# First attention in a two-block kernel: key/value groups side by side on half arrays, keys in two halves, values stationary

## What is computed

```python
def attend_blocks(q, k, v):            # q: (B, 512, 8, 64); k, v: (B, 768, 2, 64)
    ...
    scale = ATT_HEAD_DIM ** -0.5
    def one_block(qi):
        s = jnp.einsum("bqhgd,bkhd->bhgqk", qi, k, preferred_element_type=jnp.float32) * scale
        p = jax.nn.softmax(s, axis=-1)
        return jnp.einsum("bhgqk,bkhd->bqhgd", p.astype(v.dtype), v)
```

## Time and profile before

| | |
|---|---|
| median of 3 runs | 2099.91 us (2099.75 to 2102.64) |
| profiled execution | 2094.38 us, its span 2093.1 us |
| TensorE busy | 1808.2 us, 86% of the span |
| VectorE, ScalarE, GpSimd busy | 866.0, 547.3, 126.8 us |
| attention and scan stage | 155.8 to 539.9 us |
| mean granted TensorE clock | 0.958 of full speed |

### The profile page before, as it was taken

One profiled execution on the slowest core, in us unless ns is written; L12 is line 12 of the kernel. 1 busy time (PEld: TensorE's weight loads), 2 busy tenths in 40 slices (PEclk: granted clock), 3 DMA queues, 4 the chain that ended last, 5 costly groups with the idle time before them and its releaser, 6 DMA issues.

```text
span 2093.1 us, 21196 instructions
## 1 busy us (share of the span) xinstructions
PE 1808.2 (86%) x8537; PEld 1227.8 (59%) x8537; DVE 866.0 (41%) x1365; ACT 547.3 (26%) x908; POOL 126.8 (6%) x120
## 2 busy tenths in 40 slices
PE   4999889897899893888888888899788699999998
PEld 2657475766677771333232333488467678888876
DVE  4066372437733426011110111527567744444443
ACT  2134333334522313000000000232345533222221
POOL 0002120203000001000000000000000001000010
PEclk9999999998999996999999999999889899999999
DMA  9131202112104221999999999442300022232211
GB/s 348 55 109 41 82 20 101 41 72 90 41 1 167 104 98 52 384 421 421 421 422 422 421 420 420 150 156 85 121 1 1 1 81 81 82 120 81 81 41 41
DMA packets 92360, 329.44 MB, mean 157 GB/s; under 512 B 7348, under 2 KB 22632, under 8 KB 67688
## 3 DMA queue, kind: packets, MB, share of 16 engines
q1 hardware_dynamic: 84384, 312.59, 38.1%
q10 hardware_dynamic: 5928, 8.16, 1.2%
q0 software_dynamic: 1952, 7.34, 0.9%
HBM read 322.82 MB, written 4.19 MB: 156 GB/s over the span
## 4 chain that ended last, share of the span: by engine, by line
PE 66%; DMA 14%; DVE 12%; ACT 4%; issue 3%; ACTq 1%; POOL 1%; SPq 1%; DVEq 0%; POOLq 0%
PE PS L565 20%; PE PS L346 13%; PE PS L663 8%; PE PS L884 8%; DMA ring<-in_w_exp_down_dram 6%; DMA ring<-in_w_exp_gate_dram 5%; PE PS L342 3%; PE PS L534 3%; PE PS L674 2%; PE PS L729 2%; DVE wR L1415 1%; PE PS L772 1%; PE PS L426 1%; DMA ring<-in_w_mod_dram 1%; DVE mrow L1426 1%
## 5 line engine op out<-in xcount | busy, mean ns | idle before, releaser
L565 PE MATMUL PS<-hR,wR 128*128 128x512 f32 x1200 | 301.0, 410 | 30.9 <-DVE wR L1415 17.1
L565 PEld LDWEIGHTS PS<-hR,wR 128*128 128x128 f32 x1200 | 233.8, 197 | 95.6 <-issue 34.5
L663 PE MATMUL PS<-ring,xeT 128*64 128x512 f32 x1024 | 230.3, 600 | 40.3 <-DMA ring<-in_w_exp_gate_dram 38.0
L1415 DVE TENSOR_TENSOR wR<-ring,wR 128x1024 fp32r<-128x1024 f32 (+2 forms) x142 | 161.1, 1135 | 250.8 <-ACT wR L946 250.6
L946 ACT CAST wR<-ring 128x1024 fp32r<-128x1024 f32 (+2 forms) x142 | 138.3, 975 | 217.0 <-PE PS L884 126.5
L663 PEld LDWEIGHTS PS<-ring,xeT 128*64 128x64 f32 x1024 | 76.8, 138 | 192.5 <-issue 186.1
L884 PE MATMUL PS<-wR,hR 128*128 128x512 f32 x768 | 176.2, 390 | 8.9 <-DVE tmp L2097 6.9
L565 PE MATMUL PS<-xR,wR 128*128 128x512 f32 x768 | 175.3, 389 | 0.0
L884 PEld LDWEIGHTS PS<-wR,hR 128*128 128x128 f32 x768 | 143.6, 188 | 41.5 <-DVE tmp L2097 9.6
L565 PEld LDWEIGHTS PS<-xR,wR 128*128 128x128 f32 x768 | 144.1, 188 | 29.9
L663 PE MATMUL PS<-ring,hidT 128*64 128x512 f32 x512 | 115.2, 596 | 25.9 <-DMA ring<-in_w_exp_down_dram 20.0
(11 more groups left out here) (381 smaller groups left out, 2316.9 us busy)
## 6 DMA issues: line engine op xcount, KB each, us to landing
ring<-in_w_exp_gate_dram SPq DMA_DIRECT2D x64, 1024.0 KB, 13.9
ring<-in_w_exp_up_dram SPq DMA_DIRECT2D x64, 1024.0 KB, 13.7
ring<-in_w_exp_down_dram SPq DMA_DIRECT2D x64, 1024.0 KB, 11.9
ring<-in_w_mod_dram SPq DMA_DIRECT2D x12, 2048.0 KB, 8.6
ring<-in_w_in_dram SPq DMA_DIRECT2D x11, 2048.0 KB, 9.3
ring<-in_w_up_dram SPq DMA_DIRECT2D x8, 2048.0 KB, 8.3
ring<-in_w_down_dram SPq DMA_DIRECT2D x8, 2048.0 KB, 7.8
ring<-in_w_in_dram SPq DMA_DIRECT2D x9, 1024.0 KB, 5.5
```

The costliest lines, as they stand in the source:

```text
L565: mm = T.matmul(b, o[s][:, k, :], x[:, t, k, :], start=(k + j == 0), stop=(k == nk - 1 and j == 2))
L663: mm = T.matmul(b[es, ns], stat[:, 2 * kq + k, es], W.view(units[e2])[:, k, ns], start=(kq + k == 0), stop=(kq == 3 and k == 1))
L1415: V.tensor_tensor(lo, W.view(unit)[:, ks, cs], hi.bitcast(F32), ALU.subtract) \
```

## The change

Heads j of both groups now go side by side, 16 pairs instead of 32 heads. The keys lie in `kT`, both groups' channels one over the other, without zeros. Scores of a pair are two products with 64 partitions each, one on each half of the array's rows, for 384 of the keys; a second call does the other 384. VectorE takes the maxima of both heads in each half of the keys, and Exp uses the half's own maximum. `scale` then finds the smaller negative maximum, the Exp of each half's gap to it, the whole sum, its reciprocal, and scales P itself, in four pieces, before it is turned. Values are stationary (128 keys by 64 channels), turned P of two pairs moves (256 columns), one group on each half of the array's columns; the output comes with channels in partitions, so that it is copied to `oattT` at once and `ot` is gone. `oattT` has its channels in another order, and `head_cols` loads the rows of the second branch's matrix to suit, in two transfers. The attention has 66 turns again, in the order of `attention_order`.

```diff
...
@@ -104,7 +104,18 @@
 
 
 def cols(w, a, n):
-    return w[:, a:a + n].rearrange("(k p) n -> p k n", p=128), w.shape[0] // 128, n
+    k = w.shape[0] // 128
+    return [(slice(0, 128), slice(0, k), w[:, a:a + n].rearrange("(k p) n -> p k n", p=128))], k, n
+def head_cols(w, a, n):
+    parts = [(slice(64 * g, 64 * g + 64), slice(0, 4), w[256 * g:256 * g + 256, a:a + n].rearrange("(j p) n -> p j n", p=64))
+             for g in range(2)]
+    k = w.shape[0] // 128
+    if k > 4:
+        parts.append((slice(0, 128), slice(4, k), w[512:, a:a + n].rearrange("(k p) n -> p k n", p=128)))
+    return parts, k, n
 
 
 def weight_units(d):
...
@@ -119,8 +130,8 @@
                 u.append((("mod", 4 + 4 * hp + (0, 0, 0, 0, 0, 1, 2, 3)[n]),
                           *cols(d["w_mod"], 2048 + 512 * (4 * hp + what), 512)))
     u.append(("gate", *cols(d["w_in"], 2048, 512)))
-    for br, (a, wb) in enumerate(((3328, "w_branch_a"), (4352, "w_branch_b"))):
-        u += [(("wb", br), *cols(d[wb], 0, 1024)), (("mg", br, 0), *cols(d["w_in"], a, 512)),
+    for br, (a, wb, rows_of) in enumerate(((3328, "w_branch_a", cols), (4352, "w_branch_b", head_cols))):
+        u += [(("wb", br), *rows_of(d[wb], 0, 1024)), (("mg", br, 0), *cols(d["w_in"], a, 512)),
               (("mg", br, 1), *cols(d["w_in"], a + 512, 512))]
     u += [(("wo", s), *cols(d["w_out"], 512 * s, 512)) for s in range(2)]
     for p in range(8):
...
@@ -173,11 +184,10 @@
 
     m1 = Area(nc, KEEP, HT)
     oattT, oT = m1.take("oattT", [128, 4, 512]), m1.take("oT", [128, 4, 512])
-    qT, kz = m1.take("qT", [128, 4, 512]), m1.take("kz", [128, 2, 768])
-    pb = m1.take("pb", [128, 2, 768])
+    qT, kT = m1.take("qT", [128, 4, 512]), m1.take("kT", [128, 768])
+    pb, avs = m1.take("pb", [128, 2, 768]), m1.take("avs", [128, 6, 128])
     m2 = Area(nc, DYN, END)
-    avs, pT = m2.take("avs", [128, 6, 128]), m2.take("pT", [128, 2, 768])
-    ot, st = m2.take("ot", [128, 2, 512]), m2.take("st", [128, 4, 3])
+    pT, st = m2.take("pT", [128, 6, 2, 2, 128]), m2.take("st", [128, 2, 6, 2, 2])
     qh, vh = m2.take("qh", [128, 2, 512]), m2.take("vh", [128, 6, 256])
     KK, GG, LF = (m2.take(n, [128, 2, 768]) for n in ("KK", "GG", "LF"))
     lbt, reset = m2.take("lbt", [128, 6, 8]), m2.take("reset", [128, 768], U8)
...
@@ -406,7 +416,7 @@
         def turn_keys(pool):
             T.wait_ge(*dve_in["k"])
             for i in range(6):
-                b = pool.take(T, ("kT", i), act_in["kz", i])
+                b = pool.take(T, ("kT", i), act_in["kT", i])
                 turn(b[:, 0:128], akv[:, i, :]).then_inc(pe_in.sem, pe_in.up(("kT", i)))
 
         def turn_query(pool, i):
@@ -418,36 +428,34 @@
 
         def attention(pool):
             T.wait_ge(*act_in["qT", 3])
...
+            def scores(u):
+                n, kh = divmod(u, 2)
+                i, j = divmod(n, 4)
+                b = pool.take(T, ("s", u), act_att["e", u], 2)
+                for g in range(2):
+                    gs = slice(64 * g, 64 * g + 64)
+                    mm = T.matmul(b[:, 512 * g:512 * g + 384], qT[gs, j, 128 * i:128 * i + 128],
+                                  kT[gs, 384 * kh:384 * kh + 384], start=True, stop=True)
+                mm.then_inc(pe_att.sem, pe_att.up(("s", u)))
+            def turn_p(n, g):
+                b = pool.take(T, ("t", n, g), act_att["pT", n, g], 2)
+                T.wait_ge(*dve_att["sc", n])
+                for c in range(6):
+                    mm = turn(b[:, 128 * c:128 * c + 128], pb[:, g, 128 * c:128 * c + 128])
+                mm.then_inc(pe_att.sem, pe_att.up(("t", n, g)))
+            def values(n):
+                b = pool.take(T, ("v", n), act_att["o", n])
+                T.wait_ge(*act_att["pT", n, 1])
+                for c in range(6):
+                    for g in range(2):
+                        mm = T.matmul(b[64 * g:64 * g + 64, 0:256], avs[:, c, 64 * g:64 * g + 64],
+                                      pT[:, c, g].rearrange("p j q -> p (j q)"), start=(c == 0), stop=(c == 5))
+                mm.then_inc(pe_att.sem, pe_att.up(("v", n)))
+            yield from attention_order(scores, lambda n: None, turn_p, values)
 
         def scan(pool, level_pool):
             for q in range(4):
...
@@ -910,6 +918,25 @@
         select()
         ffn()
 
+    def attention_order(scores, scale, turn_p, values):
+        for n in range(17):
+            if n < 16:
+                scores(2 * n)
+            if n:
+                turn_p(n - 1, 1)
+            yield
+            if n < 16:
+                scores(2 * n + 1)
+                yield
+                scale(n)
+            if n and n % 2 == 0:
+                values(n - 1)
+            yield
+            if n < 16:
+                turn_p(n, 0)
+                yield
     def select_order(scores, compress2, compress3, mix_conv, turn_out, compressed, turn2, values2):
 
         steps = None
...
@@ -994,13 +1021,9 @@
                 A.activation(rr[:, 0:n], rr[:, 0:n], ACT.Sqrt).then_inc(s.sem, s.up(("rms", name)))
 
         def turn_keys():
-            A.wait_ge(*pool_in["kz"])
             for i in range(6):
                 A.wait_ge(*pe_in["kT", i])
-                for g in range(2):
-                    gs = slice(64 * g, 64 * g + 64)
-                    c = A.copy(kz[gs, g, 128 * i:128 * i + 128], bank(("kT", i))[gs, 0:128])
-                c.then_inc(act_in.sem, act_in.up(("kz", i)))
+                A.copy(kT[:, 128 * i:128 * i + 128], bank(("kT", i))[:, 0:128]).then_inc(act_in.sem, act_in.up(("kT", i)))
 
         def turn_query(i):
             A.wait_ge(*pe_in["qT", i])
...
@@ -1009,26 +1032,35 @@
 
         def attention():
             s = act_att
...
+            def scores(u):
+                n, kh = divmod(u, 2)
+                A.wait_ge(*dve_att["max", u])
+                if n:
+                    A.wait_ge(*pe_att["t", n - 1, 1])
+                for g in range(2):
+                    c = A.activation(pb[:, g, 384 * kh:384 * kh + 384], bank(("s", u))[:, 512 * g:512 * g + 384], ACT.Exp,
+                                     bias=st[:, n % 2, 0, kh, g:g + 1], accum_out=st[:, n % 2, 1, kh, g:g + 1])
+                c.then_inc(s.sem, s.up(("e", u)))
+            def scale(n):
+                A.wait_ge(*dve_att["gap", n])
+                A.activation(st[:, n % 2, 3], st[:, n % 2, 3], ACT.Exp).then_inc(s.sem, s.up(("gap", n)))
+            def turn_p(n, g):
+                A.wait_ge(*pe_att["t", n, g])
+                if n >= 2:
+                    A.wait_ge(*pe_att["v", n - 1 - n % 2])
+                A.copy(pT[:, :, g, n % 2, :], bank(("t", n, g))[:, 0:768].rearrange("p (c q) -> p c q", q=128)) \
+                    .then_inc(s.sem, s.up(("pT", n, g)))
+            def values(n):
+                i, j = divmod(n, 4)
+                A.wait_ge(*pe_att["v", n])
+                A.copy(oattT[:, j - 1:j + 1, 128 * i:128 * i + 128],
+                       bank(("v", n))[:, 0:256].rearrange("p (j q) -> p j q", j=2)).then_inc(s.sem, s.up(("o", n)))
+            yield from attention_order(scores, scale, turn_p, values)
 
         def scan():
             s = act_scan
...
@@ -1556,25 +1588,37 @@
 
         def attention():
             s = dve_att
...
+            def scores(u):
+                n, kh = divmod(u, 2)
+                V.wait_ge(*pe_att["s", u])
+                V.tensor_reduce(st[:, n % 2, 0, kh, :], bank(("s", u)).rearrange("p (g x) -> p g x", g=2)[:, :, 0:384], AX,
+                                ALU.max, negate=True).then_inc(s.sem, s.up(("max", u)))
+            def scale(n):
+                neg, total, low, gap, part, r = (st[:, n % 2, x] for x in range(6))
+                V.wait_ge(*dve_att["max", 2 * n + 1])
+                V.tensor_tensor(low[:, 0, :], neg[:, 0, :], neg[:, 1, :], ALU.min).then_inc(s.sem, s.up())
+                V.wait_ge(*s.last)
+                V.tensor_tensor(gap, low[:, 0:1, :].broadcast_to([128, 2, 2]), neg, ALU.subtract) \
+                    .then_inc(s.sem, s.up(("gap", n)))
+                V.wait_ge(*act_att["gap", n])
+                V.tensor_tensor(part, gap, total, ALU.mult).then_inc(s.sem, s.up())
+                V.wait_ge(*s.last)
+                V.tensor_tensor(low[:, 1, :], part[:, 0, :], part[:, 1, :], ALU.add).then_inc(s.sem, s.up())
+                V.wait_ge(*s.last)
+                V.reciprocal(low[:, 1, :], low[:, 1, :]).then_inc(s.sem, s.up())
+                V.wait_ge(*s.last)
+                V.tensor_tensor(r, gap, low[:, 1:2, :].broadcast_to([128, 2, 2]), ALU.mult).then_inc(s.sem, s.up())
+                V.wait_ge(*s.last)
+                for g in range(2):
+                    for kh in range(2):
+                        p = pb[:, g, 384 * kh:384 * kh + 384]
+                        V.tensor_scalar(p, p, r[:, kh, g:g + 1], None, ALU.mult).then_inc(s.sem, s.up())
+                s.also(("sc", n))
```

(15 more changed lines are left out.)

69 lines of the change are left out of this document (removed).

## The result

| | before | after |
|---|---|---|
| median, 9 runs each | 2099.75 us (2096.45 to 2102.74) | 2107.38 us (2105.14 to 2112.91) |
| ratio, with its 95% interval | | 1.0039 (1.0028 to 1.005) |
| profiled execution | 2094.38 us, span 2093.1 | 2107.76 us, span 2106.5 |
| attention and scan stage | 155.8 to 539.9 us | 158.9 to 557.7 us |
| mean granted clock | 0.958 | 0.951 |

What follows compares the result with a forecast made beforehand. It took TensorE, with VectorE 2.0 us behind, to bound the level stretches, and chains over all engines between them. Terms -10.0 + 2.7 + 2.0 + 3.5 + 2.4 - 1.8 - 0.6 - 1.0 gave 2.8 slower, 2102.7 us; range 2088 to 2118, own case 2096 to 2108.

Steps and rivals of the forecast that it cites:

- Level stretches: Four stretches of seven scan levels beside attention: VectorE's added work makes each 2.5 us slower, 10 in all.
- earlier outputs: After the last level, scores replace P turn and values, so the scan's outputs start earlier: 2.3 to 2.7 us faster.
- `scale`, priced 2.8 us: VectorE's step per pair: six small operations 1.1, ScalarE round trip 0.35, four scalings 1.3; bounds 2.4 and 4.0 us.
- Rival 3: TensorE's clock falls to half behind waits of about 2.4 us in the levels: 12 us slower, 2115; chance 0.15.
- Gate projections: Second projection of passes 2 and 3 no longer waits for banks that ScalarE must empty: 3.9 us faster each.
- Pass 2, 3, 4: Net change of the parts between level stretches, projections included: 2.0, 3.5 and 2.4 us faster.
- bank ring: Six banks followed through the new order: the second gate projection meets banks of outputs or finished scores.
- Pass 1: Earlier second scores delay ScalarE's chunk-key Exps by some 2.6 us, states win back 0.8: 1.8 us slower.
- rival 1: TensorE's whole relief counts, VectorE not bounding the levels: 32 us faster, 2068; chance 0.07.
- Rival 2: `scale` fits, a level stretch costing 0.5 us instead of 2.5: 8 us less, 2095; chance 0.20.
- Rival 4: Row halves of scores don't overlap, 0.64 us more for each of 32: 5 us slower, 2108; chance 0.13.
- End: At the attention's end, last values and one copy replace values, scaling, turn and copy: 0.6 us slower.

Runs made afterwards that it cites:

- experiment 1: The changed kernel without the four scalings of P in `scale`, so P stays unnormalised: 2092.26 us, 0.9967 of before.
- experiment 4: The changed kernel with the four scalings of P done by ScalarE straight behind its Exp of the gaps: 2100.92 us, 1.0012 of before.
- experiment 9: The changed kernel with ScalarE scaling P, a turn later for the eight pairs in level stretches, at once for the others: 2090.38 us, 0.9959 of before.
- experiment 7: The changed kernel without GpSimd's subtractions and their Exps for the last five of seven levels in each pass: 2096.88 us, 0.9995 of before.
- experiment 5: The changed kernel with useless TensorE products around the wait for scaled P, in the level stretches' eight pairs: 2104.71 us, 1.0031 of before.
- experiment 6: The changed kernel with both products of a scores call on the same half of the rows: 2120.09 us, 1.0108 of before.
- experiment 3: The kernel before without the maximum, Exp taking a fixed scale: 2091.2 us, 0.9968 of before.
- experiment 10: The kernel of experiment 9 with scan ahead of attention on VectorE and ScalarE in each pass's first-level turn: 2092.61 us, 0.9977 of before.
- experiment 2: The changed kernel without any maximum or gaps, Exp taking a fixed scale: 2085.51 us, 0.9933 of before.

## Why the prediction was right, and what was off

The forecast was slower by 2.8 us (2102.7); measured 7.6 slower, 2107.4, at the upper end of the forecast's own range of 2096 to 2108. The direction was right, and so was the place of the loss. Its size was not, and that the median still lies in the range is in part luck: for the stage the terms add up to 1.8 us slower, and in the profiles it lost 14.7; that the medians are only 7.6 apart comes from outside the stage, where no term of the prediction stands for it. The steps:

- **Level stretches, "2.5 slower, four times, 10".** That VectorE's added work costs the stretches is shown by experiments 1, 4 and 9, which take the scalings off it. The size didn't hold: 17.1 us net of the earlier outputs, where the terms gave 10.0 - 2.7 = 7.3. The mis-sized term is **`scale`, priced 2.8 us**: the eight in the stretches took 28.1 us instead of 22.4. The four scalings were right (1.32 from first start to the next instruction, against 1.3). The six small operations with the round trip, priced at 1.45, took 1.40 in the two `scale` that GpSimd left alone and 1.41 to 1.49 in experiment 7; in the other six they took 2.14 to 2.90. So the row behind the price, a reciprocal of 0.19, priced an undisturbed VectorE rightly, and what it left out is GpSimd. Experiment 7 shows that by taking GpSimd away. The range's upper end gave the collision to the scalings, which did not meet it (all 64 took 410 to 422 ns), and its 4.0 us was passed twice, by 4.22 and 4.23.
- **The rest of the levels' loss, some 4 us,** is idle time that was to be used up. VectorE was to be busy 95% or more; it was 89, 89, 93 and 89%. Its busy time rose from 90.5 to 106.6 us, 16.1 where 4 x 3.8 = 15.2 were priced (`scale` took more, the level products lost 3 less to GpSimd). But its idle time, which was to fall to some 0.7 a stretch, went from 10.7 to 11.8 us, and 7.5 of that are waits for TensorE's level products. The two engines hold each other up: TensorE has new waits on P and merged levels (21.2 us in the stage, 5.1 of it outside the levels) and runs products at 1.2 GHz behind them. I expected a clock of 1.00 and TensorE 75% busy; it was 0.85 to 0.94 and 27.0 us busy of 30.2, 89%, in part since work at half clock counts as busy. Rival 3 was a part of the truth, at 2 to 3 us of the second halves (experiment 5) and not at 12. Its condition, a wait of about 2.4 us, was not what decided: the level at 216.14 is slow behind waits of 0.71 and 0.99, a first level of experiment 6 took 3.78 us behind a wait of 1.57, and in experiment 3 all four first levels took 2.05 behind waits of 1.75 to 2.09. What the slow first levels cost isn't separated; no kernel with the new attention had them fast in passes 1 and 2.
- **Gate projections, "3.9 faster each".** Right: 236.88 - 225.90 = 10.98 us from the first to the second, with no wait for ScalarE, predicted 11.0; in pass 3 also 10.98.
- **Pass 2, 3, 4: predicted 2.0, 3.5, 2.4 faster**; the parts between gave 1.4, 1.5 and 2.7. Missed ahead of the levels of passes 3 and 4: TensorE waits for scaled P ahead of the states (2.09 us at 410.89, 3.00 at 511.10), the new wait that `scale` leaves outside the levels, and a mod product waits 5.70 us at 487.61 for a bank whose scores ScalarE still reads; the bank ring had been followed to "finished scores".
- **Pass 1, "1.8 slower".** 3.06. The chunk keys came 18.75 us after the first scores instead of 16.51, 2.2 later against 2.6 priced; the states were to win back 0.8 and won nothing, since the first level waits 4.67 us instead of 1.29, a wait that I had not looked for. It ends with the level's Exp; that this one stands behind attention's Exps is under 1 us of it (experiment 10).
- **TensorE's forms.** Scores 0.85 (0.84 predicted), values 2.81 (3.3), maxima 0.95 (0.96). TensorE's relief at full clock is 32 x 0.45 + 32 x 1.34 - 8 x 2.81 + 2 = 37 us, more than the 32 of rival 1. Its busy time in the stage fell by 16; the rest I put down to work at a lower clock (0.95 before, 0.90 after). What came to the end of it is the 5.7 us of experiments 2 and 3, and that only without maxima. Rival 1 is out.
- **Rival 2** (`scale` fits in the idle time) is out: 17 us of levels. **Rival 4** (no overlap) is out by experiment 6.
- **End, "0.6 slower"**: 0.13. The "1.0 slower" for weight loads elsewhere is shown by no run; what changed outside the stage is within its scatter.

Open: more than half of experiment 6's time; what first levels at full clock would be worth; what before would gain without GpSimd's subtractions, which no run shows (its TensorE was busy in the levels throughout, so I expect little); and why the medians are 7.6 us apart where the stage of the profiles lost 14.7.

## What to carry to other kernels

Before moving work from TensorE to VectorE, look at what VectorE's new instructions read and at who runs beside them at that moment. Here every operation with two operands in SBUF, however small, could cost up to a whole GpSimd instruction more; the one-tensor scaling of P escaped in the changed kernel and doubled in experiment 2, by timing alone. The reciprocal of one element and the reduction from PSUM kept their own time. A price from a row of an undisturbed instruction is a lower bound, and the upper one is that row plus the other engine's instruction. When a shared engine is the bound in one kind of stretch and idle in the other, choose the engine of a movable step by the stretch: one placement for all took 2101 or 2111 us, the mixed one 2090.

## What was not expected of the hardware

- An operation on 2 or 4 elements a partition with two operands in SBUF: 0.15 to 0.16 us alone, 0.79 to 1.03 in the rows above when GpSimd's 1.04-us subtraction had started. A product of 512 elements: 0.68 alone, up to 1.74. The scaling of 768 elements of one tensor, SBUF to SBUF: 0.62 alone, up to 1.46 (experiment 2).
- A reduction from PSUM: 0.93 to 0.96 beside GpSimd and alone. A reciprocal of one element: in after no reciprocal ran beside GpSimd, but in before ten of 32 did and took 0.14 to 0.16 like the others, as here in a timeline of both engines:

```profile
198.71 1.04 POOL L2160 TENSOR_TENSOR X<-GG 128x512 f32<-128x512 f32 x1
...
198.81 0.14 DVE L1570 RECIPROCAL st<-st 128x1 f32<-128x1 f32 x1
```

- Two products on opposite halves of the rows, 64x384 each: 0.92 us recorded for the call, 0.85 from start to start; on one half 1.55.
- Values with 64 stationary columns on both halves of the columns: 24 passes of 256 in 2.81 us, 0.117 each, faster than the 0.137 of the nearest row before.
- TensorE at 1.2 GHz for all or most of the products behind a wait of 3.7 to 4.7 us in every pass of after (3.06 to 3.79 us for 1.95), and again after short waits that follow each other (0.71 and 0.99 us ahead of the 3.54 at 216.14). Products put into those gaps kept it at 1.95.
